# One decoder layer on one core: eight products of high weights, then eight of low weights

## The reference, cut to what matters

```python
h = jnp.einsum('bsd,de->bse', x, w_in)
q, k, v, z_attn, u_pool, z_pool, g_pre = jnp.split(h, idx, axis=-1)
for g, (window, dilation) in enumerate(DILATED_GROUPS):      # (128,1), (512,4), (2048,16)
    o_g, lse_g = dilated_window_attention(q[:, :, g], k[:, :, g], v[:, :, g], window, dilation)
...
y_attn = o.astype(x.dtype) * jax.nn.silu(z_attn)
y_pool = causal_pool_mixer(u_pool, w_pool, pool_scale) * jax.nn.silu(z_pool)
merged = g_attn * jnp.einsum('bsc,cd->bsd', y_attn, w_proj_attn) \
    + g_pool * jnp.einsum('bsc,cd->bsd', y_pool, w_proj_pool)
out = jnp.einsum('bsd,de->bse', merged, w_out)
return layer_norm(DEEPNORM_ALPHA * x + out, ln_gamma, ln_beta)
```

## Time and profile before

| | |
|---|---|
| Median of three runs | 941.01 us |
| Span of the profiled execution, first to last instruction | 939.3 us |
| TensorE busy | 932.3 us, 99% |
| TensorE weight loads | 812.1 us, 86% |
| VectorE busy | 634.1 us, 68% |
| ScalarE busy | 420.2 us, 45% |
| Mean granted TensorE clock | 0.999 of full speed |
| HBM read | 175.85 MB, 189 GB/s over the span |

### The profile page before, as it was taken

How to read it: one execution, slowest core, us unless ns; L and a number is a source line. 1 busy time by engine, 2 the same in 40 slices (tenths; PEclk the granted TensorE clock), 3 DMA queues, 4 the chain that set the end, 5 groups by cost and what they waited for, 6 DMA issues and landing times.

```text
span 939.3 us, 13719 instructions
## 1 busy us (share of the span) xinstructions
PE 932.3 (99%) x5190; PEld 812.1 (86%) x5190; DVE 634.1 (68%) x1007; ACT 420.2 (45%) x589; POOL 0.2 (0%) x4
## 2 busy tenths in 40 slices
PE   9999999999999999999999999999999999999997
PEld 7888888888888888888888889888888888888887
DVE  6767657666777567557666778666666666666866
ACT  6444444444434344444444444545445454444340
POOL 0000000000000000000000000000000000000000
PEclk9999999999999999999999999999999999999999
DMA  9745554544545545554544546655545555557432
GB/s 374 266 156 180 199 188 145 209 164 165 207 152 185 185 168 174 198 185 156 197 166 181 193 166 224 224 180 210 192 179 186 178 217 179 184 193 297 179 135 90
DMA packets 26416, 178.58 MB, mean 190 GB/s; under 512 B 3327, under 2 KB 3583, under 8 KB 5759
## 3 DMA queue, kind: packets, MB, share of 16 engines
q1 hardware_dynamic: 25920, 173.72, 51.6%
q10 hardware_dynamic: 452, 4.24, 1.2%
HBM read 175.85 MB, written 2.10 MB: 189 GB/s over the span
## 4 chain that ended last, share of the span: by engine, by line
PE 98%; DVE 1%; DMA 0%; ACT 0%; DVEq 0%; issue 0%
PE proj_ps L411 39%; PE proj_ps L417 20%; PE attn_ps L411 7%; PE attn_ps L403 4%; PE attn_ps L404 4%; PE attn_ps L405 4%; PE attn_ps L417 3%; PE value_ps L405 3%; PE value_ps L404 3%; PE value_ps L403 3%; PE mixed_ps L404 1%; PE mixed_ps L403 1%; PE mixed_ps L405 1%; PE mixed_ps L540 1%; PE proj_ps L454 1%; PE attn_ps L484 1%
## 5 line engine op out<-in xcount | busy, mean ns | idle before, releaser
L411 PE MATMUL proj_ps<-xt,w_hi 128*128 128x512 f32 x1600 | 557.1, 392 | 0.0
L417 PE MATMUL proj_ps<-xt,w_lo 128*128 128x256 f32 x1600 | 445.5, 280 | 0.0
L839 DVE TENSOR_TENSOR w_lo<-w_raw,w_hi 128x1024 fp32r<-128x1024 f32 x314 | 369.3, 1220 | 83.0 <-ACT w_hi L682 82.6
L411 PEld LDWEIGHTS proj_ps<-xt,w_hi 128*128 128x128 f32 x1600 | 298.3, 187 | 65.1
L682 ACT ACTIVATE w_hi<-w_raw 128x1024 fp32r<-128x1024 f32 x314 | 313.6, 1051 | 59.8 <-PE mixed_ps L405 25.1
L417 PEld LDWEIGHTS proj_ps<-xt,w_lo 128*128 128x128 f32 x1600 | 302.3, 189 | 1.4
L702 ACT ACTIVATE corr<-proj_ps 128x256 f32<-128x256 f32 x102 | 39.1, 383 | 280.8 <-PE proj_ps L417 278.2
L853 DVE TENSOR_TENSOR qk_f<-proj_ps,corr 128x256 f32<-128x256 f32 x46 | 19.5, 423 | 73.0 <-ACT corr L702 73.0
L411 PE MATMUL attn_ps<-yp,w_hi 128*128 128x512 f32 x128 | 45.1, 391 | 0.0
L411 PE MATMUL attn_ps<-ya,w_hi 128*128 128x512 f32 x128 | 45.1, 391 | 0.0
L405 PE MATMUL value_ps<-w_hi,xt 128*128 128x512 f32 x96 | 37.4, 390 | 0.0
(11 more groups left out here) (178 smaller groups left out, 917.8 us busy)
## 6 DMA issues: line engine op xcount, KB each, us to landing
w_raw<-in_weights SPq DMA_DIRECT2D x158, 1024.0 KB, 4.8
first_raw<-in_first SPq DMA_DIRECT2D x8, 640.0 KB, 8.3
res<-in_x_rows ACTq DMA_DIRECT2D x1, 2048.0 KB
out_rows<-res SPq DMA_DIRECT2D x8, 256.0 KB, 2.1
gamma<-in_gamma_row ACTq DMA_DIRECT2D x1, 1024.0 KB
beta<-in_beta_row ACTq DMA_DIRECT2D x1, 1024.0 KB
mask<-in_mask SPq DMA_DIRECT2D x1, 512.0 KB, 17.7
ident<-in_identity SPq DMA_DIRECT2D x1, 64.0 KB, 17.5
```

What stands on the lines that cost most here:

```text
L411: mm(bank, w_hi[:, slot, k * P:(k + 1) * P], tile.rearrange("p a s -> p (a s)"), start=first, stop=False)
L417: done = mm(bank[:, SEQ:2 * SEQ], w_lo[:, slot, k * P:(k + 1) * P], tile[:, 0, :], start=False, stop=last)
L839: tt(w_lo[:, slot, cols], w_raw[:, slot, cols], w_hi[:, slot, cols].bitcast(F32), ALU.subtract).then_inc(lo_split, 1)
```

## The change

Two constants change. `A_TOGETHER` and `B_TOGETHER` go from 1 to `HALF`, which is 8:

```diff
-FIRST_TOGETHER, A_TOGETHER, B_TOGETHER = 2, 1, 1
+FIRST_TOGETHER, A_TOGETHER, B_TOGETHER = 2, HALF, HALF
```

## The result

The changed kernel takes 944.25 us (943.95 to 945.10, six runs) against 941.15 us (940.32 to 941.69, six runs) before: a ratio of 1.0029, 95% interval 1.0017 to 1.0042. It is slower by 3.1 us, 0.3%, and the interval is clear of 1. The forecast was 941.5 us and "no change that can be measured", with 944.3 us as the middle of the first rival; the range of 940.0 to 945.0 holds the result, the forecast itself missed it by 2.8 us. (Two details ahead of the prediction are wrong: the weight stream has 161 chunks, 97 and 48 and 16, not 162; and the product shown in the earlier trace rows is the first of that chunk, which reads the high weights, the first low one standing behind it. Nothing hangs on either.)

A forecast was written before the change was run, and what follows sets the result against it. TensorE, never waiting at full clock, was taken to bound the kernel by its products back to back. Span 939.3 + 1.8 (turns) - 1.3 (slow rhythm) = 939.8, plus 1.7 to the median: 941.5 us; range 940.0 to 945.0.

The forecast's parts named there:

- rival 1: First three highs of each of 228 halves: turns cost more than they seem, +3.3 us, 944.3; shares 32% with rival 2.
- The bound: Whole span, 939.3 us: TensorE 99% busy at full clock, so time is the sum of products back to back.
- The first order: Changed chunks: eight pairs cost 2.774 us alternating or in rows of one kind, so the change is worth nothing.
- The waits at 0: Ahead of each half and its lows: the removed and the added split wait each cost 0, as splits are far ahead.
- The slow rhythm, -1.3 us,: Head 4's first six chunks and six chunks behind transposes: 0.0065 us a pair extra goes if grouping breaks it, -1.3 us.
- The turns, +1.8 us,: Size changes between lows and highs in 228 cycles of eight and eight: 8 ns each, +1.8 us.
- the near end: Lower bound taken for a turn there and back: 3.3 ns, from the three chunks by twos.
- far end: Upper bound taken for the 8 ns: 12 ns, what the turn out of the lows leaves net before rounding.
- the third term: Four lows ahead of a row of 512s: 0.47 us in place of 0.48, a credit of 0.01 us.
- The range's upper end: Whole kernel: 945.0 us, given as rival 1 at its middle, some 22 ns a cycle.
- Rival 2: Lows in a row 3 ns dearer, highs unchanged: +4.8 us, 945.8, or 944.5 without slow rhythm; shares 32% with rival 1.
- Rival 3: Rows pay nothing and turns gain 0.02 us a cycle: -4.6 us, with -1.3 this is 935.1 us; 8%.

The follow-up runs named there:

- 5: Against the kernel before: low products of 512 columns instead of 256, alternating order kept; 1139.61 us.
- 6: Against the alternating kernel with 512-column low products: the same products grouped eight and eight; 1139.45 us.
- kernel 1: Against the changed kernel: grouped by eight, but with the single wait for the low split ahead of each half, as before the change; 944.11 us.
- kernel 8: Against the kernel before: alternating, but nine first halves grouped by eight (behind each head's transposes, and head 4's first chunk); 946.40 us.
- kernel 9: Against the kernel before: only the chunk behind the transposes grouped, by twos, fours, eights, sixteen or mixed in heads 0 to 6; 947.87 us, one run.
- 11: Against kernel 10: head 3's chunk by eights, first chunk of each of the gate stage's four loop turns by sixteens; 944.96 us.
- 7: Against the kernel before: only the gate stage's 48 chunks grouped by eight, heads alternating; 943.27 us.
- 12: Against kernel 10: head 3's chunk by sixteens, first chunk of each of the gate stage's four loop turns by twos; 940.64 us.
- kernel 10: Against the kernel before: chunk behind the transposes by sixteens in heads 0, 1, 2, 4, 5, 6 and by twos in head 3; 940.65 us.

## Why the prediction was right and wrong

The result lies in the range because the range took in rival 1, not because the forecast held.

- **The bound** was right: a sum of products back to back, at full clock, without waits.
- **The first order** was right: a long row of each kind costs what the alternating pair costs. With equal sizes (kernels 5 and 6) the order is free to within 0.2 us.
- **The waits at 0** were right: kernel 1 shows it.
- **The slow rhythm, -1.3 us,** was right in size: 228 turns at 20 ns make 4.56 us, the changed chunks lengthened by 3.14, which leaves -1.4. That it keeps itself up once it has started is what kernels 8, 9 and 11 show. It went because no changed chunk alternates any more; a grouped half alone does not end it (kernel 8).
- **The turns, +1.8 us,** are the step that failed. That turns cost time was right, the size was not: 20 ns a cycle instead of 8, +4.6 us instead of +1.8. This alone moves 941.5 to 944.3. I took the 3.3 ns of the chunks by twos as the near end, though a row of two is over before the five late highs have passed. My far end of 12 ns was short too: to the nanosecond it is the turns of the earlier trace rows, where three highs are late by 20 together and two lows early by 8, while in the changed kernel a fourth and a fifth high are late as well, by 5.4 and 4.3. And the third term that I set against it, four lows ahead 0.01 us early, is no part of a turn: behind the first two, lows in a row of eight keep 120 ns. The highs of the earlier trace rows had it in view: there the start stayed uneven for nine products.
- **Rival 1** came true, by its own signs too: a cycle of 2.793 us with the first three highs at 0.70. That its 944.3 us is the measured time to 0.1 is in part luck: it has three highs late by 20 ns together and nothing given back, the trace has five late by 28 and two lows early by 7. The range's upper end, 945.0, is 23 ns a cycle by the terms of the sum, not 22, and rival 1's middle is 20.
- **Rival 2** (lows dearer, highs unchanged) is out: from the sixth on highs keep 226.7 ns, and lows 120. **Rival 3** is out: the two early lows give back 7 ns, a quarter of what the highs lose.

The Trainium skill (TensorE: Matmul & The Clock Gate, Back-to-back issue gap) gives an isolated gap of N/2.4 + 2.5 ns, by size alone: 216 and 109 ns. The trace has 226.7 and 120.0 in long rows, so this fp32r stream pays 13.3 ns a product beyond N/2.4; and beside that it has a term of order that the formula has not, 20 ns a turn or 6.5 ns a pair.

**What stays open.** Why a product of another size sets the next five off their pace is not settled; the ends of products in the profile are modelled, so that only their starts can be read, and no run changed the number of weight loads. That the upper level of the kernel before is its gate stage in the slow rhythm is inferred and not seen in a profile of such a run. For it: the step between the medians of the levels is 4.8 to 5.4 us, and 768 x 6.5 ns is 5.0; three kernels that fix the entry or the order of the gate stage (7, 11, 12) had one level in 36 runs; and kernel 9's trace shows the stage at that pace. A rival with the same step is that the stretches in the heads are the slow ones, as in kernel 8. Two kernels speak against it: kernel 7 left the heads as they were and had no upper run in twelve, when the kernel before had ten of 22 beside it; and kernel 10 gave the heads fast entries, left the gate stage as it was, and still had one run of twelve at 945.67 us.

## What to carry to other kernels

When TensorE never waits, count turns between product sizes: here each turn from eight or more products of 256 columns to as many of 512 and back cost 20 ns, so either alternate strictly or make the rows long; of the lengths run, four was the worst. Look at the pace of identical stretches in the order of time; two paces of the same code mean that what stands ahead of the stretch is worth changing, and one short, fixed entry in a loop may remove a second level from a kernel's times. Try more than one entry: by twos it fixed the lower level here, by sixteens the upper one. Do not size a transient by a row that is shorter than it, or by one place of the trace: it held for three products in the earlier trace rows, nine in the earlier trace rows and five in the changed kernel.

## What was not expected of the hardware

- The alternating order has two lasting paces at the same clock, 0.3467 and 0.3532 us a pair of 512 and 256 columns, over up to 768 pairs (266.25 and 271.36 us).
- Rows of four and four cost more than rows of two, eight or sixteen: 947.01 us against 942.91, 944.25 and 942.36.
- What stood ahead of a loop with unchanged entry was worth 5.1 us in it (the gate stage of kernel 9, 271.36 us against 266.25), and the times of one unchanged kernel lay on two levels 5 us apart; that the second comes from the first is inferred.
